# Loads of value pages and expert weights reordered in a fused decoder step

## The reference

```python
h = rmsnorm(x)
rq, rk, rv, rg, aq, ak, av, gr, ga = split(h @ w_in)       # 8192 columns
r = retention(rope(rq), rope(rk), rv) ; r = silu(rg) * group_norm(r) ; r = r @ w_ret_o
a = moba(rope(aq), keys, values)                             # 8 heads of 128
a = a @ w_att_o
x = x + (sigmoid(gr) * r + sigmoid(ga) * a) @ w_o
h = rmsnorm(x)
combine = weights of the top 2 of 8 experts in the top 1 of 4 groups
x = x + sum_e (silu(h @ w_gate[e]) * (h @ w_up[e]) * combine[:, e]) @ w_down[e]   # 32 experts, 1024x256
y = rmsnorm(x)
```

## Time and profile before

| | |
|---|---|
| median of 3 runs | 768.91 us (768.21 to 770.3) |
| the profiled execution, its own time | 769.54 us |
| its span, first to last instruction | 767.7 us |
| PE busy | 653.7 us (85%) |
| DVE / ACT / POOL busy | 308.1 / 141.3 / 139.2 us |
| moved by DMA | 243.00 MB, mean 317 GB/s |

### The profile page before, as it was taken

One profiled execution on the slowest core, in us unless ns is written; L12 is line 12 of the kernel. 1 busy time (PEld: TensorE's weight loads), 2 busy tenths in 40 slices (PEclk: granted clock), 3 DMA queues, 4 the chain that ended last, 5 costly groups with the idle time before them and its releaser, 6 DMA issues.

```text
span 767.7 us, 13776 instructions
## 1 busy us (share of the span) xinstructions
PE 653.7 (85%) x5037; PEld 459.7 (60%) x5037; DVE 308.1 (40%) x1554; ACT 141.3 (18%) x404; POOL 139.2 (18%) x209
## 2 busy tenths in 40 slices
PE   6999999999899987989998999827996848767593
PEld 4888887787788765744433877626654525443341
DVE  3005988998867775610000221444324201111114
ACT  3222223223235222210010000121110101000012
POOL 0169954761000223200000000011000000000000
PEclk9999999999999999999999999958998969787898
DMA  9939899789978999579999989457699999999971
GB/s 306 273 110 321 284 305 393 263 280 354 360 252 269 338 322 350 171 276 402 399 410 383 291 330 381 174 225 266 245 392 401 388 387 401 402 403 399 415 283 58
DMA packets 93830, 243.00 MB, mean 317 GB/s; under 512 B 8786, under 2 KB 54482, under 8 KB 85442
## 3 DMA queue, kind: packets, MB, share of 16 engines
q1 hardware_dynamic: 56818, 192.99, 67.1%
q10 hardware_dynamic: 31328, 32.00, 12.8%
q0 software_dynamic: 5616, 17.11, 6.5%
HBM read 235.00 MB, written 9.11 MB: 318 GB/s over the span
## 4 chain that ended last, share of the span: by engine, by line
PE 55%; DMA 26%; DVE 14%; issue 2%; SPq 1%; ACT 1%; POOL 0%; DVEq 0%; ACTq 0%; POOLq 0%
PE zps L885 31%; DVE kall L1367 7%; DMA qb<-in_w_down 6%; DMA hT<-in_w_down 6%; PE zps L1202 4%; PE nps L1179 4%; PE nps L1054 4%; DMA ring_all<-in_w_ret_o 4%; DMA ring_all<-in_w_down 3%; DMA out<-sfin 2%; PE nps L856 2%; DMA kall<-in_cache_k 2%; DMA gain<-v_rows 2%; PE zps L856 1%; PE bps L1217 1%
## 5 line engine op out<-in xcount | busy, mean ns | idle before, releaser
L885 PE MATMUL zps<-hT,ring_all 128*128 128x264 f32 x1152 | 276.3, 394 | 1.6 <-DVE hT L1548 1.0
L885 PEld LDWEIGHTS zps<-hT,ring_all 128*128 128x128 f32 x1152 | 218.3, 194 | 45.6 <-issue 5.6
L1367 DVE CUSTOM_DVE_ANT_0 kall<-kall,qb 128x128 f32<-128x128 f32 x512 | 153.2, 366 | 59.8 <-DMA kall<-in_cache_k 57.1
L596 POOL DMA_INDIRECT zatt<-h_rows,tidx_i x16 | 15.1, 943 | 361.3 <-DVEq L1636 199.8
L1054 PE MATMUL nps<-ring_all,zret 128*64 128x512 f32 x256 | 59.1, 600 | 5.4 <-DMA ring_all<-in_cache_v 4.3
L885 PE MATMUL zps<-headT,ring_all 128*128 128x264 f32 x256 | 58.5, 388 | 4.9 <-DMA ring_all<-in_w_ret_o 3.5
L885 PEld LDWEIGHTS zps<-headT,ring_all 128*128 128x128 f32 x256 | 48.2, 190 | 16.0 <-issue 6.0
L1709 DVE TENSOR_TENSOR qdT<-qdT,nps 128x64 f32<-128x64 f32 x32 | 7.1, 221 | 118.6 <-ACT qdT L801 118.1
L645 ACT ACTIVATE zt<-zps 128x264 f32<-128x264 f32 x56 | 21.8, 390 | 153.6 <-PE zps L885 147.5
L1535 DVE TENSOR_TENSOR hT<-zps,zatt 128x264 f32<-128x264 f32 x8 | 3.5, 433 | 96.4 <-PE zps L885 96.3
L1367 DVE DVE_READ_ACCUMULATOR2_ANT scores<- 128x1 f32 x512 | 40.9, 80 | 0.0
(11 more groups left out here) (360 smaller groups left out, 829.1 us busy)
## 6 DMA issues: line engine op xcount, KB each, us to landing
kall<-in_cache_k SPq DMA_DIRECT2D x64, 512.0 KB, 6.5
ring_all<-in_cache_v SPq DMA_DIRECT2D x64, 512.0 KB, 8.1
ring_all<-in_w_in ACTq DMA_DIRECT2D x26, 1024.0 KB, 8.4
ring_all<-in_w_gate SPq DMA_DIRECT2D x12, 1024.0 KB, 18.8
ring_all<-in_w_up SPq DMA_DIRECT2D x12, 1024.0 KB, 21.8
ring_all<-in_w_down SPq DMA_DIRECT2D x12, 1024.0 KB, 14.5
ring_all<-in_w_in SPq DMA_DIRECT2D x6, 1024.0 KB, 13.5
kall<-in_w_gate SPq DMA_DIRECT2D x5, 1024.0 KB, 22.6
```

The costliest lines, as they stand in the source:

```text
L596: pool.indirect_dma_start(out=rows, out_offset=None, in_=h2_rows, in_offset=bass.IndirectOffsetOnAxis(ap=col, axis=0), bounds_check=T - 1, ...
L885: mm = pe.matmul(zps[m % 2][:, 0:T], w[:, k, P * fb:P * (fb + 1)], rhs[:, k, :], start=(k == 0), stop=(k == KT - 1))
L1367: ins = v.tensor_tensor_reduce(kh, kh, qb[b % 2][:, P * h:P * (h + 1)], 1.0, 0.0, ALU.mult, ALU.add, scores[:, pg, AH * b + h:AH * b + h + 1])
```

## The change

1. Value units 0 to 3 (`V_SOON` = 4, eight pages, 4 MB) leave the ring. Units 2 and 3 are loaded into the two halves of `zdec_all` right behind key page 53, after waits on four semaphores that say that its old contents are used. Units 0 and 1 are loaded into the two halves of `kall` behind all key pages, when key pages 61 and 63 are used. The ring's list shrinks from 76 units to 72, so each unit behind `ret_o` 0 stands four places earlier. Gate and up of sets 2 and 3 wait on `v_used`, not on the key pages.
2. Both halves of `quad_down` stand one expert later (e % 4 is 1 and 2, not 0 and 1), and so do `ADD_AT`, the copies on ACT, and the residual.
3. SP issues down of expert e - 4 behind gate and up of e while e is below 16, then of e - 2. So from expert 6 on the order is gate/up 6, 7, 8, 9, 10, down 6, gate/up 11, down 7 and on to gate/up 15, down 11, then gate/up 16, downs 12, 13, 14, then alternating as before.
4. The downs of experts 28 to 31 are loaded in two halves of the columns, all first halves ahead of all second halves, behind one wait for quad 6's products. The second halves share the semaphore `d_last`, for which only the last `quad_down` waits.
5. Behind the last expert, PE makes the samples' rows first, ACT squares the samples in place of DVE, and DVE scales them into another buffer.

The core of the diff (renamed turn semaphores and the loop for overfull experts, which no row shows running, are left out):

```diff
@@ -39,7 +39,7 @@
 NQUAD = NE // 4
-ADD_AT = {(q, half): 4 * q + 5 + half + 2 * (q == 0) for q in range(NQUAD - 1) for half in range(2)}
+ADD_AT = {(q, half): 4 * q + 6 + half + 2 * (q == 0) for q in range(NQUAD - 1) for half in range(2)}
 EDGES = (T - 1) // CAP
...
@@ -112,6 +112,7 @@
 N_V = NB * NPG // 2
+V_SOON = 4
 KRING = 4
...
@@ -120,7 +121,7 @@
         order.append(("ret_o", j))
-        order += [("v", k) for k in range(N_V) if min(k // 8, 2) == j]
+        order += [("v", k) for k in range(V_SOON, N_V) if min(k // 8, 2) == j]
     order = [u for u in order if u != ("ret_o", 3)] + [("ret_o", 3)]
...
@@ -248,6 +249,7 @@
         rt = zr[:, 4096:6144]
+        v_soon = [kall[:, 0:2048], kall[:, 2048:4096], zdec_all[:, 0:2048], zdec_all[:, 2048:4096]]
         xg = [zflat[0:2 * CAP, DM * i:DM * (i + 1)] for i in range(2)]
...
@@ -404,6 +407,12 @@
+            def value_pages(j, out, signal):
+                for k in range(2):
+                    pid = sp.value_load(ptab[0:1, 2 * j + k:2 * j + k + 1], min_val=0, max_val=NPOOL - 1)
+                    sp.dma_start(out[:, DM * k:DM * (k + 1)],
+                                 cache_v[0, bass.ds(pid, 1)].rearrange("o s h d -> (o s) (h d)")).then_inc(signal, 16)
+
             for n, (kind, j) in enumerate(UNITS):
...
@@ -411,16 +420,23 @@
                     slot_free(n)
-                    for k in range(2):
-                        pid = sp.value_load(ptab[0:1, 2 * j + k:2 * j + k + 1], min_val=0, max_val=NPOOL - 1)
-                        sp.dma_start(ring[n % RING][:, DM * k:DM * (k + 1)],
-                                     cache_v[0, bass.ds(pid, 1)].rearrange("o s h d -> (o s) (h d)")).then_inc(slot_in[n % RING], 16)
+                    value_pages(j, ring[n % RING], slot_in[n % RING])
                 else:
...
                         key_page(p)
+                        if p == 53:
+                            sp.wait_ge(f_nT, 1)
+                            sp.wait_ge(out_done, 96)
+                            sp.wait_ge(d_T, 1)
+                            sp.wait_ge(v_out, 16)
+                            for j in (2, 3):
+                                value_pages(j, v_soon[j], v_soon_in[j])
+                    for j in range(2):
+                        sp.wait_ge(page_done, NB * NPG - 2 + 2 * j)
+                        value_pages(j, v_soon[j], v_soon_in[j])
...
@@ -432,13 +448,9 @@
-            sp.wait_ge(page_done, NB * NPG)
+            sp.wait_ge(v_used, 2)
             gate_up_in(2, 2)
-            sp.wait_ge(f_nT, 1)
-            sp.wait_ge(out_done, 96)
-            sp.wait_ge(d_N, 1)
-            sp.wait_ge(d_T, 1)
-            sp.wait_ge(v_out, 16)
+            sp.wait_ge(v_used, V_SOON)
             gate_up_in(3, 3)
...
@@ -462,13 +474,25 @@
             down_in(5, 5)
-            for e in range(SETS, NE + 2):
-                if e < NE:
-                    sp.wait_ge(e_GU, e + 1 - SETS)
-                    gate_up_in(e % SETS, e)
-                if e >= SETS + 2:
-                    sp.wait_ge(e_D, 2 * ((e - 2 - SETS) // 4 + 1))
-                    down_in((e - 2) % SETS, e - 2)
+            def next_down(e):
+                sp.wait_ge(e_D, 2 * ((e - SETS) // 4 + 1))
+                down_in(e % SETS, e)
+
+            downs = SETS
+            for e in range(SETS, NE):
+                sp.wait_ge(e_GU, e + 1 - SETS)
+                gate_up_in(e % SETS, e)
+                while downs <= min(e - (4 if e < 16 else 2), NE - 5):
+                    next_down(downs)
+                    downs += 1
+            for e in range(downs, NE - 4):
+                next_down(e)
+            sp.wait_ge(e_D, 2 * ((NE - 1 - SETS) // 4 + 1))
+            for half, signals in enumerate((d_in, None)):
+                for e in range(NE - 4, NE):
+                    sp.dma_start(down_w[e % SETS].rearrange("p (f n) -> p f n", f=FB)[:, :, 512 * half:512 * (half + 1)],
+                                 w_down[0, bass.ds(e, 1), :, 512 * half:512 * (half + 1)].rearrange("o (f p) n -> p (o f) n", p=P)
+                                 ).then_inc(signals[e % SETS] if signals else d_last, 16)
...
@@ -814,15 +838,15 @@
-            for e in range(NE + 2):
-                if e < NE:
-                    silu(e % 2, e + 1)
-                if e >= 4 and e % 4 < 2:
-                    y_copy(nps[0] if e == NE + 1 else zps[1], slice(0, P), e % 4, 2 * (e // 4 - 1) + e % 4 + 1)
-                if e < NE:
-                    h_copy(e % 2, e // 4, e % 4, e + 1, 2 * (e // 4 - 1) if e >= 8 else None)
-                if e % 4 == 2 and e < NE:
+            for e in range(NE):
+                silu(e % 2, e + 1)
+                if e >= 5 and e % 4 in (1, 2):
+                    y_copy(zps[1], slice(0, P), e % 4 - 1, 2 * (e // 4 - 1) + e % 4)
+                h_copy(e % 2, e // 4, e % 4, e + 1, 2 * (e // 4 - 1) if e >= 8 else None)
+                if e % 4 == 2:
                     pick_copy(e // 4, P, e // 4 + 1)
+            for half, bank in enumerate((zps[1], nps[0])):
+                y_copy(bank, slice(0, P), half, 2 * NQUAD - 1 + half)
             act.wait_ge(t_exp, 1)
...
@@ -833,15 +857,19 @@
                     act.wait_ge(e_C, j + 3)
-                    act.sem_inc(act_turn, 1)
-
-            act.wait_ge(e_C, 1)
-            act.activation(fbuf[0], accs[0][:, :], ACT.Square, accum_out=st[:, 12:13]).then_inc(f_sq, 1)
-            act.wait_ge(e_C, 2)
-            act.activation(ring[5][:, 0:DM], accs[1][:, :], ACT.Square, accum_out=st[:, 13:14]).then_inc(f_sq, 1)
+                    act.wait_ge(e_Sc, j * 2 + (2 * NQUAD + 2))
+                    act.sem_inc(past_wait, 1)
+
+            act.wait_ge(t_exp, 1)
+            act.wait_ge(e_Sc, 2 * NQUAD)
+            act.activation(fsq, xs[0:NB, 2, :], ACT.Square, accum_out=st[0:NB, 14:15]).then_inc(f_sq, 1)
+            for t in range(2):
+                act.wait_ge(e_C, t + 1)
+                act.activation((fbuf[0], ring[5][:, 0:DM])[t], accs[t][:, :], ACT.Square,
+                               accum_out=st[:, 12 + t:13 + t]).then_inc(f_sq, 1)
             act.wait_ge(f_root, 1)
             act.activation(fbuf[2], xs[:, 0, :], ACT.Copy, scale=st[:, 9:10]).then_inc(o_x[0], 1)
-            act.activation(fsam, xs[0:NB, 2, :], ACT.Copy, scale=st[0:NB, 11:12]).then_inc(o_x[2], 1)
+            act.activation(fsam, fbuf[1][0:NB, :], ACT.Copy, scale=st[0:NB, 11:12]).then_inc(o_x[2], 1)
             act.wait_ge(o_x[2], 1)
...
@@ -1045,14 +1073,19 @@
             def values(j):
-                n = AT["v", j]
                 b = j // 4
-                pe.wait_ge(slot_in[n % RING], slot_value(n))
+                if j < V_SOON:
+                    pages = v_soon[j]
+                    pe.wait_ge(v_soon_in[j], 32)
+                else:
+                    n = AT["v", j]
+                    pages = ring[n % RING]
+                    pe.wait_ge(slot_in[n % RING], slot_value(n))
                 for k in range(2):
...
                         mm = pe.matmul(nps[0][64 * c:64 * (c + 1), :], pw[:, 512 * p + 64 * b:512 * p + 64 * (b + 1)],
-                                       ring[n % RING][:, DM * k + 512 * c:DM * k + 512 * (c + 1)],
+                                       pages[:, DM * k + 512 * c:DM * k + 512 * (c + 1)],
                                        start=(j == 0 and k == 0), stop=(j == N_V - 1 and k == 1))
...
@@ -1250,6 +1283,8 @@
                 last = q == NQUAD - 1 and half == 1
+                if last:
+                    pe.wait_ge(d_last, 64)
                 if y_n[0] and not last:
...
@@ -1264,8 +1299,8 @@
                     pair_x(e // 2 + 1)
-                if e >= 4 and e % 4 < 2:
-                    quad_down(e // 4 - 1, e % 4)
+                if e >= 5 and e % 4 in (1, 2):
+                    quad_down(e // 4 - 1, e % 4 - 1)
                 h_tr(e % 2, e + 1)
...
@@ -1276,18 +1311,18 @@
                     tile_rows()
-                if e == 6:
+                if e == 7:
                     residual_in()
...
             pe.wait_ge(e_Dc, 2 * NQUAD - 1)
+            sample_rows(zps[1], q, 0, P)
             add_rows(0, q, 0, P)
             pe.wait_ge(e_Dc, 2 * NQUAD)
+            sample_rows(nps[1], q, 1, P)
             add_rows(0, q, 1, P).then_inc(e_C, 1)
-            sample_rows(zps[1], q, 0, P)
-            sample_rows(nps[1], q, 1, P)
             add_rows(1, q, 0, P)
...
@@ -1752,26 +1788,25 @@
                     v.wait_ge(e_pickT, j + NQUAD)
-                    v.sem_inc(dve_turn, 1)
+                    v.sem_inc(past_wait, 1)
                     shape = [P, 6, CAP]
...
                     v.wait_ge(e_selx, j + 1)
-                    v.sem_inc(dve_turn, 1)
+                    v.sem_inc(past_wait, 1)
                     v.tensor_tensor(pick[0][:, :, 0:CAP], selx[:, 0:3, :], selx[:, 3:6, :], ALU.add).then_inc(e_pick, 1)
...
                     v.wait_ge(e_C, j + 3)
-                    v.sem_inc(dve_turn, 1)
```

(10 more changed lines are left out.)

20 lines of the change are left out of this document (11 added, 9 removed).

## The result

The changed kernel takes **762.53 us** (median of 9 runs, 759.95 to 765.2) against 768.21 us for the kernel before (median of 9 runs) on the same chip: a ratio of 0.991, 95% interval 0.9888 to 0.9932. The forecast was 753.2 us, 746 to 762. The direction was right; the gain was less than half of the one forecast, and the time lies just outside the range.

What follows compares the result with a forecast made beforehand. No single engine bounds the whole: DMA is full in the value stage, with PE nearly full, and in the experts from 550 us. Terms sum to -15.7 us: 769.5 to 753.8 profiled, 753.2 us median; range 746 to 762.

Steps and rivals of the forecast that it cites:

- they fill holes: Key stage: the 2 MB added behind key page 53, 5.2 us of DMA work, fit a stretch with share 0.67.
- the two covers in the experts: Loads covering DMA during waits: 10.4 us against 10.8 at expert 16, 5.2 against 5.8 ahead of the last downs.
- Key stage, -2.5: Key stage: a shorter wait for the state update's row broadcast gains 2 us, the clock 0.5; between -4 and +3.
- Values, -5: Value stage: 4 MB less to load, PE becomes the bound; gain 5 us, bounds 0 and -7.8.
- The hole, -6.4: Start of the experts, 541 to 549 us: gate/up 9 and 10 fill the DMA idle, gaining all 6.4 us.
- Expert 16, +1: Experts, where down 14 waits for quad 2: DMA idle for 0 to 2 us, 1 us given back.
- The end, -2: Last downs: stream broken 0.6 us, PE's part behind the last byte 1.8 us instead of 5.4; between -3.5 and +3.
- The norm tail, -0.8: Behind the final adds: moving the samples' square off DVE brings the norm's scalars from 8.8 to 7.9 us.
- Rival B: Experts: stream cut at down 14 and ahead of the last 4 MB, +1 becomes +4, -2 becomes +1; 759 us, chance 0.13.
- A: Rival, value stage: the ring starves and refills at 10 us a round, gain 1 us, not 5; 757 us, chance 0.14.
- C: Rival, experts: a full queue holds SP, so loading four ahead does nothing; 760 us, chance 0.04.
- D: Rival, key stage: the last ten key pages land late, 2 us a page, 20 us in all; 773 us, chance 0.05.

Runs made afterwards that it cites:

- e9: The changed kernel with PE taking the 28 ring value units first and the four outside the ring last; ratio 0.9903 to the kernel before.
- e13: The kernel before with only gate and up loaded four ahead of the downs up to expert 15, two from there; 764.14 us, ratio 0.9904.
- e5: The changed kernel run once more with nothing changed; ratio 0.9911 to the kernel before.
- e2: The changed kernel with value units 2 and 3 loaded after the last key page, not behind key page 53; ratio 0.9855 to the kernel before.
- e3: The changed kernel with the last four downs loaded whole behind the same single wait, no column halves; ratio 0.9921 to the kernel before.

## Why the prediction was wrong, step by step

Of the 15.7 us of the sum 7.3 came in the profile. What is missing is 2.7 us in the key stage, 1.6 at the values, 3.6 in the experts (0.4 at the hole, 1.4 at expert 16 and 2.1 at the end, less 0.3 won in between) and 0.4 behind them. The direction was right; the steps that failed are the key stage's "they fill holes", the loss of stream at the values, the two covers in the experts, and PE's part at the end.

- **Key stage, -2.5: +0.2 in the profile, +0.4 in the mean.** The mechanism of the gain was right: the states' wait fell by 2.5 us. That this equals the term is in part luck, for the term was 2 us of one wait and 0.5 us of clock. The step that failed is "they fill holes": it followed the key pages, which are used 19.8 us behind their issue, and no other transfer in flight there. The store had no time to spare; DVE waited 1.6 us for it already before. The forecast named "up to 2 us" as a possible price and left it out of the sum; 2.2 us were measured. The Trainium skill, page "DMA: Bandwidth & Descriptors", section "Issuing engines are not separate DMA queues", says that DMAs of all issuers run on the same 16 engines and interleave, and gives no price. The store agrees: it landed 17.5 us behind its issue instead of 14.6 when SP's loads filled the windows.
- **Values, -5: -3.4 in the profile, -3.0 in the mean of eleven.** PE's cap and the idle DMA were right (4 to 6 us, 5.0). The mis-sized term is the loss of stream: the forecast added 4 to 6 us to 73 us of loads, and 8.5 were lost by the bytes, since behind the gap it had 2.6 us for each MB at once and the ring refilled at 335 to 360 GB/s for 20 us. The rate is not all of it: e9, with the stream full, took back only 1 us.
- **The hole, -6.4: 6.0 us in bytes, 4.2 us in time when alone (e13).** "All of it, since the stream is full to 735 us" holds for DMA. It left out that PE, not DMA, ended the kernel, which the forecast itself had read from the earlier trace rows: a gain in the stream counts only as far as PE's last wait moves, 5.0 us in e13, and PE then took 0.8 us longer.
- **Expert 16, +1: 2.4 by the bytes.** The place and cause were right; the idle is 1.2 us by the shares, and again the rate around it is low (338 GB/s over 20 us against 383). In e13, with the old quads, 1.2 us are lost by the same count of bytes.
- **The end, -2: about 0.** Two of its terms failed. The first is the cover, "DMA then still has gate/up 31, 2 MB or 5.2 us". From 724 to 728 us the windows move 2 x 225 + 2 x 61 KB, 0.6 MB, and from 723.27 to 724 another 0.3: gate/up 31 was more than half in when 30 landed. The cover was some 2 us and the break 3, and the last 4 MB landed 14.0 us behind their first issue (726.99 to 741.0), where the forecast had 12.4. So the stream lost 1.7 us of its lead, where 0.6 stood in the sum. The second is PE's part, 5.4 us less 1.8. It took the median landing of two loads for the last one; behind the last landing 4.2 us passed before and 2.6 pass now, 1.6 us less instead of 3.6. PE's path to the last issue was right, 3.7 us from 723.27 to 726.99 (3.8 forecast).
- **The norm tail, -0.8: -0.4 here, -1.4 in e5 and every other version of it** (15.8 to 16.0 us against 17.2 to 17.4). In the changed kernel's profile the granted clock fell from full speed (1.00 from 741 to 742 us) to 1.2 GHz, about 1 us behind PE's last wait for a load, and that made the part behind the adds about 1 us longer (the first two matmuls took 1.91 us, 1.02 in e5). The wait alone does not explain it: it was 2.2 us here, 3.2 in e5 and 2.4 in e2, and in those two the clock stayed at 1.00. What sets it off stays open.

```profile
743.00:744.00 1.00, 1.00 (x8) 0.14 (x1) 0.00 (x0) 0.06 (x1) 0.00 (x0) 0.50 0.00 0
```

Rival B came true in both its places, at 1.4 us more than the sum had at the first and 2 at the second (B's own prices were 3 us more at each), with the key stage's gain gone and the values 2 us short besides. The text called both covers thin and gave B 0.13; it put the high end at B without the key stage, 761.7, and nothing of the values' shortfall into it. A's slow refill was there at about half its price. C and D were judged rightly, but D looked at the very place where the key stage lost, and asked only after key pages. By the signs that the forecast named, the waits of PE at the values are 5.1 us, where it asked for less than 4, and the stream is cut for 1.2 and 2.9 us behind 550 us, more than the 3 at which it called itself wrong; the window below 0.8 at the values is there (0.61), and `ret_out(0)` did not start earlier.

## What to carry to other kernels

Before a load is moved into a stretch with a share of 0.7, list every transfer in flight there and who waits for it; the slack of the loads beside it says nothing of a store behind which an engine stands. Count what covers a wait in bytes not yet landed, not in loads not yet released: of several large loads issued together, the last is partly in when the first lands. Where several loads are issued in a row, read the landing of the last and not the median. And compare two versions of a DMA-bound stage by a ledger of bytes from a common mark; a share of 1 can hide a tenth of the rate (360 GB/s for 404 here).

## What the runs showed of the hardware

A share of 1.01 went with 360 GB/s at 360 us, and one of 1.05 with 426 in the rows below. Column halves with rows of 2 KB landed at 366 GB/s at a share of 1.03 from 730 to 736 us (and at 407 from 736 to 738), the whole downs of e3 with rows of 4 KB at 408 to 426 at 1.01 to 1.05, in the same place of the kernel. The changed kernel first:

```profile
730.00:736.00 6.00, 5.29 (x71) 2.75 (x68) 0.90 (x2) 0.45 (x2) 0.00 (x0) 1.00 1.03 366
```

```profile
730.00:732.00 2.00, 2.00 (x59) 1.64 (x57) 0.68 (x1) 0.00 (x0) 0.00 (x0) 1.00 1.05 426
732.00:734.00 2.00, 1.29 (x8) 0.71 (x7) 0.22 (x1) 0.45 (x2) 0.00 (x0) 1.00 1.01 408
```

Over 730 to 738 us that is 376 against 416 GB/s, or 1.1 us more for 4 MB (an estimate from these two rates); no such difference is seen in when the last load landed, so what the short rows cost the kernel stays open. And one and the same key stage moved the start of `ret_out(0)` by up to 6.5 us from profile to profile (322.2 to 328.7 us), which is as much as the whole change brings; what makes it stays open.
